# Feed-forward matmuls of 362 columns over three PSUM banks instead of 272 columns over two

## What is computed

```python
for l in range(DEPTH):                                   # 2 layers
    xp = xp + 0.5 * swiglu(rms_norm(xp, ffn1_norm[l]), *f1)
    ...                                                  # even or odd mixer
    xp = xp + 0.5 * swiglu(rms_norm(xp, ffn2_norm[l]), *f2)
# swiglu(h, gate, up, down) = (silu(h @ gate) * (h @ up)) @ down, with 1024 x 2816 and 2816 x 1024 weights
```

## Time and profile before

| | |
|---|---|
| time, 3 runs | 2167.08 us median, 2164.73 to 2167.14 |
| span of the profiled execution (the page records no time beside it) | 2169.2 us |
| TensorE busy | 2121.6 us, 98% |
| VectorE, ScalarE, GpSimd busy | 1028.8, 690.9, 274.7 us |
| chain that ended last: TensorE's share | 92%, line 646 87% |
| matmuls, each with a weight load | 16662 |

### The profile page before, as it was taken

One profiled execution on the slowest core, in us unless ns is written; L12 is line 12 of the kernel. 1 busy time (PEld: TensorE's weight loads), 2 busy tenths in 40 slices (PEclk: granted clock), 3 DMA queues, 4 the chain that ended last, 5 costly groups with the idle time before them and its releaser, 6 DMA issues.

```text
span 2169.2 us, 41417 instructions
## 1 busy us (share of the span) xinstructions
PE 2121.6 (98%) x16662; PEld 2040.0 (94%) x16662; DVE 1028.8 (47%) x1300; ACT 690.9 (32%) x908; POOL 274.7 (13%) x290
## 2 busy tenths in 40 slices
PE   9999999999999999999999999999988899999997
PEld 8999999997999999999999999999844799999997
DVE  6442444567654324455442444656835364424443
ACT  5221222237254212224441222222334244412221
POOL 0000111300310000021000001403145320000012
PEclk9999999999999999999999999999999999999999
DMA  3222432222132222222222222322589322222221
GB/s 143 87 96 79 131 108 94 91 69 73 69 107 89 91 83 88 89 93 71 86 102 83 78 90 96 112 91 83 153 236 267 117 85 87 102 82 78 87 100 68
DMA packets 68710, 218.65 MB, mean 101 GB/s; under 512 B 10186, under 2 KB 22645, under 8 KB 68544
## 3 DMA queue, kind: packets, MB, share of 16 engines
q1 hardware_dynamic: 58864, 191.00, 26.2%
q0 software_dynamic: 9184, 24.80, 4.1%
q10 hardware_dynamic: 576, 1.67, 0.2%
HBM read 212.67 MB, written 5.78 MB: 101 GB/s over the span
## 4 chain that ended last, share of the span: by engine, by line
PE 92%; DVE 3%; ACT 1%; DMA 1%; issue 1%; SPq 1%; DVEq 0%; ACTq 0%
PE ps L646 87%; PE ps L1067 1%; DVE rinv L1543 1%; DMA keys<-pool_kt 1%; DVE w_lo L1533 1%; PE ps L1094 1%; SPq L523 0%; PE ps L999 0%; ACT prob L1311 0%; DMA x<-xT 0%; PE ps L974 0%; PE ps L665 0%; PE ps L949 0%; PE ps L986 0%; PE ps L960 0%
## 5 line engine op out<-in xcount | busy, mean ns | idle before, releaser
L1210 ACT ACTIVATE w_hi<-raw 128x1024 fp32r<-128x1024 f32 (+2 forms) x298 | 334.8, 1124 | 1181.4 <-PE ps L646 1173.4
L646 PE MATMUL ps<-hx_hi,w_hi 128*128 128x272 f32 x3376 | 702.6, 289 | 5.1 <-DVE w_lo L1533 2.9
L646 PE MATMUL ps<-hx_hi,w_lo 128*128 128x272 f32 x3376 | 699.5, 289 | 0.0
L646 PE MATMUL ps<-hx_lo,w_hi 128*128 128x272 f32 x3376 | 696.9, 288 | 0.0
L646 PEld LDWEIGHTS ps<-hx_hi,w_hi 128*128 128x128 f32 x3376 | 531.8, 188 | 9.9 <-issue 5.8
L646 PEld LDWEIGHTS ps<-hx_lo,w_hi 128*128 128x128 f32 x3376 | 531.5, 189 | 0.0
L646 PEld LDWEIGHTS ps<-hx_hi,w_lo 128*128 128x128 f32 x3376 | 527.8, 189 | 0.0
L1533 DVE TENSOR_TENSOR w_lo<-raw,w_hi 128x1024 fp32r<-128x1024 f32 (+2 forms) x298 | 421.1, 1413 | 97.0 <-ACT w_hi L1210 96.7
L646 PE MATMUL ps<-hid_hi,w_hi 128*128 128x272 f32 x1408 | 291.1, 288 | 0.0
L646 PE MATMUL ps<-hid_lo,w_hi 128*128 128x272 f32 x1408 | 290.9, 288 | 0.0
L646 PE MATMUL ps<-hid_hi,w_lo 128*128 128x272 f32 x1408 | 290.8, 288 | 0.0
(11 more groups left out here) (315 smaller groups left out, 1516.5 us busy)
## 6 DMA issues: line engine op xcount, KB each, us to landing
raw<-gu SPq DMA_DIRECT2D x175, 512.0 KB, 3.2
raw<-down SPq DMA_DIRECT2D x64, 704.0 KB, 4.0
keys<-pool_kt SPq DMA_DIRECT2D x128, 144.0 KB, 4.5
vals<-pool_v POOLq DMA_DIRECT2D x128, 128.0 KB, 4.7
raw<-odd_in SPq DMA_DIRECT2D x21, 512.0 KB, 3.2
raw<-even_in SPq DMA_DIRECT2D x14, 512.0 KB, 3.2
raw<-even_out SPq DMA_DIRECT2D x8, 512.0 KB, 3.2
raw<-odd_out SPq DMA_DIRECT2D x8, 512.0 KB, 3.9
```

Of the source, the lines that this page charges most:

```text
L646: last = pe.matmul(acc[slot][0:m, a, 0:TH], w, r[:, t, a * TH:(a + 1) * TH], start=(begin and t == tiles[0] and one == 0), stop=((end if s ...
L1210: act.activation(w_hi[slot][:, 0:cols], raw[slot][:, 0:cols], ACT.Copy).then_inc(w_hi_done, 1)
```

## The change

The upper and the lower input lie side by side in one tile of 1088 columns (`hx`, `hid`, `mix`, `cq`). In the feed-forwards `wide_panel` replaces `panel`: the upper weights are multiplied with these 1088 columns in three matmuls of 362, 362 and 364 columns over three banks, the lower weights with the 544 upper columns in two of 272 as before. The sum of upper weights times lower input, and the lower weights' share of the second half of the tokens, thus end in columns of their own ("lower"), and are added when the accumulator is read: 180 columns of the second bank and 364 of the third (6 for slot 0, 7 for slot 1). For gate and up ScalarE copies the lower sum to SBUF (`copy_low`, two activations), VectorE adds upper and lower, and `rinv` is applied in passes of its own: to `gate`, and to `silu` in place of `up`. For a down panel VectorE adds to x in three passes (`wide_add_to_x`). The mixers keep `panel`, with the same matmuls, on the joined tiles. The distance matmul of the first feed-forward moves from bank 7 to bank 4 and waits for the first root.

```diff
+BANK = 512
+PIECE = 362
...
-        hx_hi = place("hx_hi", [P, DT, T], F32R)
-        hx_lo = place("hx_lo", [P, DT, T], F32R)
+        hx = place("hx", [P, DT, 2 * T], F32R)
+        hx_hi, hx_lo = hx[:, :, 0:T], hx[:, :, T:2 * T]
...
+        pieces = [(ps[:, 2 * s, BANK - PIECE:BANK], ps[:, 2 * s + 1, 0:PIECE], ps[:, 6 + s, 0:2 * T - 2 * PIECE]) for s in range(2)]
+        upper = [ps_flat[:, (2 * s + 1) * BANK - PIECE:(2 * s + 1) * BANK - PIECE + T] for s in range(2)]
+        lower = [(ps[:, 2 * s + 1, T - PIECE:PIECE], ps[:, 6 + s, 0:2 * T - 2 * PIECE]) for s in range(2)]
+        LOWER = 2 * PIECE - T
...
+            def wide_panel(n, slot, rhs, tiles, wait_input=None, begin=True, end=True, first=False):
...
+                one, two, three = pieces[slot]
+                for t in tiles:
...
+                    pe.matmul(one, hi, rhs[:, t, 0:PIECE], start=opens, stop=False)
+                    pe.matmul(two, hi, rhs[:, t, PIECE:2 * PIECE], start=opens, stop=closes)
+                    pe.matmul(three, hi, rhs[:, t, 2 * PIECE:2 * T], start=opens, stop=False)
+                    pe.matmul(one[:, 0:TH], lo, rhs[:, t, 0:TH], start=False, stop=closes)
+                    last = pe.matmul(three[:, T + TH - 2 * PIECE:2 * T - 2 * PIECE], lo, rhs[:, t, TH:T], start=False, stop=closes)
...
-                        panel(n0, n0 % 2, hx_hi, hx_lo, range(DT), split_input, first=(f == 0))
+                        wide_panel(n0, n0 % 2, hx, range(DT), split_input, first=(f == 0))
...
                 pe.wait_ge(rel_landed, 32)
-                pe.matmul(ps[:, 7, 0:3 * WIN], rel[:], onehot[:], start=True, stop=True).then_inc(dist_ready, 1)
+                pe.wait_ge(rms_done, stat(0))
+                pe.matmul(ps[:, 4, 0:3 * WIN], rel[:], onehot[:], start=True, stop=True).then_inc(dist_ready, 1)
...
+            def copy_low(out, n, slot, done):
+
+                act.wait_ge(panel_done, n + 1)
+                act.activation(out[:, 0:LOWER], lower[slot][0], ACT.Copy)
+                act.activation(out[:, LOWER:T], lower[slot][1], ACT.Copy).then_inc(done, 1)
...
                 act.wait_ge(prod_ready, 1)
                 act.activation(hid_hi[:, 0, :], prod[:], ACT.Copy).then_inc(hid_hi_done, 1)
-                act.wait_ge(acc_read, 3)
+                copy_low(gate_low, 2, 0, gate_low_done)
+                act.wait_ge(gate_ready, 2)
                 act.activation(silu[:], gate[:], ACT.Silu).then_inc(silu_done, 1)
+                copy_low(up_low, 3, 1, up_low_done)
...
                     def tile(i, cols):
+                        copy_low(gate_low, n0 + 2 * i, n0 % 2, gate_low_done)
                         split_hi(n0 + 2 * i + 2, n0 % 2, cols)
-                        act.wait_ge(acc_read, n0 + 2 * i + 1)
+                        act.wait_ge(gate_ready, h0 + i + 1)
                         act.activation(silu[:], gate[:], ACT.Silu).then_inc(silu_done, 1)
+                        copy_low(up_low, n0 + 2 * i + 1, (n0 + 1) % 2, up_low_done)
...
+            def gathered(out, low, n, slot, low_done, count):
+
+                dve.wait_ge(low_done, count)
+                dve.tensor_tensor(out[:], upper[slot], low[:], ALU.add).then_inc(acc_read, 1)
+                dve.wait_ge(acc_read, n + 1)
+
+            def scale_silu(h):
+
+                dve.wait_ge(silu_done, h + 1)
+                dve.tensor_tensor(silu[:], silu[:], rinv[:], ALU.mult).then_inc(silu_scaled, 1)
+                dve.wait_ge(silu_scaled, h + 1)
+
+            def wide_add_to_x(n, slot, m, factor, k):
...
+                dve.scalar_tensor_tensor(out=xm, in0=upper[slot], scalar=factor, in1=xm, op0=ALU.mult, op1=ALU.add).then_inc(x_upper, 1)
+                dve.wait_ge(x_upper, k + 1)
+                dve.scalar_tensor_tensor(out=xm[:, 0:LOWER], in0=first, scalar=factor, in1=xm[:, 0:LOWER], op0=ALU.mult, op1=ALU.add)
+                dve.scalar_tensor_tensor(out=xm[:, LOWER:T], in0=second, scalar=factor, in1=xm[:, LOWER:T], op0=ALU.mult, op1=ALU.add)\
+                   .then_inc(acc_read, 1)
...
-                        dve.wait_ge(panel_done, n0 + 2 * i + 1)
-                        dve.tensor_tensor(halves(gate[:]), acc_of(n0 % 2), halves(rinv[:]), ALU.mult).then_inc(acc_read, 1)
+                        gathered(gate, gate_low, n0 + 2 * i, n0 % 2, gate_low_done, h0 + i + 1)
+                        dve.tensor_tensor(gate[:], gate[:], rinv[:], ALU.mult).then_inc(gate_ready, 1)
                         split_lo(n0 + 2 * i + 2, n0 % 2, cols)
-                        dve.wait_ge(panel_done, n0 + 2 * i + 2)
-                        dve.tensor_tensor(halves(up[:]), acc_of((n0 + 1) % 2), halves(rinv[:]), ALU.mult).then_inc(acc_read, 1)
-                        dve.wait_ge(silu_done, h0 + i + 1)
-                        dve.wait_ge(acc_read, n0 + 2 * i + 2)
+                        scale_silu(h0 + i)
+                        gathered(up, up_low, n0 + 2 * i + 1, (n0 + 1) % 2, up_low_done, h0 + i + 1)
                         dve.tensor_tensor(prod[:], up[:], silu[:], ALU.mult).then_inc(prod_ready, 1)
```

More of the change, by code:

```diff
@@ L696, in ffn @@
                         for s in range(2):
-                            panel(n0 + 2 * i + s, (n0 + s) % 2, hx_hi, hx_lo, range(DT))
+                            wide_panel(n0 + 2 * i + s, (n0 + s) % 2, hx, range(DT))
                     if f == 0 and c == 0:
@@ L703, in hidden @@
                         pe.wait_ge(hid_done, done + t + 1)
[L704 to L705 removed]
+                    wide_panel(n1, n1 % 2, hid, range(FT), hidden)
+                    wide_panel(n1 + 1, (n1 + 1) % 2, hid, range(FT))
                     with pe.Fori(1, DT // 2) as i:
                         for s in range(2):
[L708 removed]
+                            wide_panel(n1 + 2 * i + s, (n1 + s) % 2, hid, range(FT))
             def mixer_out_begin(start, tiles, pieces, which=(0, 1)):
@@ L713, in mixer_out_begin @@
                 for t in which:
-                    panel(start + t, (start + t) % 2, mix_hi, mix_lo, tiles, end=False)
+                    panel(start + t, (start + t) % 2, mix, tiles, end=False)
             def mixer_out(start, early, late, pieces, token_halves=(0, 1)):
@@ L897, in even @@
                     if k < 0:
-                        panel(n, n % 2, hx_hi, hx_lo, range(DT), split_input if t == 0 else None)
+                        panel(n, n % 2, hx, range(DT), split_input if t == 0 else None)
                     else:
-                        panel(n, n % 2, hx_hi, hx_lo, range(DT // 2), end=False)
+                        panel(n, n % 2, hx, range(DT // 2), end=False)
                         unit_score(k)
@@ L903, in even @@
                             unit_values(k - 2)
-                        panel(n, n % 2, hx_hi, hx_lo, range(DT // 2, DT), begin=False)
+                        panel(n, n % 2, hx, range(DT // 2, DT), begin=False)
                         if k >= 1:
@@ L1164, in split_cq @@
                         pe.wait_ge(cq_done, t + 1)
-                    panel(n, n % 2, cq_hi, cq_lo, range(QT), split_cq if h == 0 else None)
+                    panel(n, n % 2, cq, range(QT), split_cq if h == 0 else None)
                     if h == 0:
```

109 lines of the change are left out of this document (64 added, 45 removed).

## The result

| | before | after |
|---|---|---|
| median | 2165.9 us (4 runs, 2164.3 to 2167.14) | 2192.71 us (4 runs, 2188.89 to 2195.16) |
| span of the profiled execution | 2169.2 us | 2193.2 us |

The ratio is 1.0117, 95% interval 1.0096 to 1.0139: the changed kernel is slower by 1.2%, where I had forecast 0.8% faster, and 16 us above the range.

A forecast was written before the change was run, and what follows sets the result against it. TensorE, 98% busy, was taken as the bound. Fewer matmuls saving 25.1 us and stalls adding 7.3 us gave -17.8 us off the median of 2167.08, so 2149.3 us; range 2143 to 2177.

The forecast's parts named there:

- The count and the place: Whole kernel: TensorE is the bound; 2112 feed-forward tiles each go from six matmuls to five with the same 1632 columns.
- Slack in the loops: Steady gate and up panels: the added VectorE and ScalarE work costs nothing, with 2.2 us to spare.
- the down panels' three passes: Down panels: one VectorE pass of 0.72 us becomes three, about 1.6 us, within 8.3 us, costing nothing.
- I take the first: Feed-forward tiles: 11.9 ns fixed per matmul, so one fewer saves 25.1 us over 2112 tiles; chance 0.48.
- a wide matmul that starts off a good address: Wide feed-forward matmuls: one costing more than its columns would make the prediction wrong; no size or chance given.
- rival 1: Feed-forward matmuls: cost is per column, nothing saved, stalls left, 2174.4 us; slower from 165.8 ns per wide matmul; chance 0.23.
- Rival 2: Feed-forward matmuls: mostly per column, small fixed part; at 3 ns 6.3 us saved, 2168.1 us; chance 0.20.
- rival 3: Feed-forward matmuls: none follows the last in under 125.2 ns; 100.3 us saved, 2074 us; chance 0.06.
- (a): First feed-forward, run-in: panel 2's read waits behind product, `hid_hi` and `copy_low`; TensorE stalls about 2.6 us.
- (b): Start of the other three feed-forwards: an add goes before the scaling, TensorE waits longer for `w_lo`; 2.5 us in all.
- (c): Last down panel of the first three feed-forwards: later x delays `hx_lo` for the next panel; 1.3 us in all.
- (d): End of the kernel: the chain runs through the last, longer add to x; 0.9 us.

## Why the prediction was wrong, step by step

**The count and the place.** 2112 tiles, five matmuls instead of six, TensorE the bound: right. Slack in the loops, the down panels' three passes: right, no steady panel waits.

**The price of a matmul: wrong, and nearly the whole miss.** The step was "I take the first", a fixed 11.9 ns per matmul and columns at 2.4 GHz, tile 739.3. Measured is 759.9. The tile was to lose 11.9 ns and gained 7.7: 19.6 ns x 2112 = 41.4 us, against a miss of 2192.7 - 2149.3 = 43.4. Counted from 739.3 the error is 20.6 ns and has two parts; 1 ns of it is that the tile before measures 752.2, not 751.2. The other 2 us of the miss lie in the stalls, the mixers and the spread between executions.

- *Mis-sized fixed part.* It is some 2.5 ns (0 to 3), the rest of the 11.9 is about 0.45 ns per column instead of 0.417. That lifts 739.3 to 746.2, 14.6 us. I had split 125.2 ns with nothing but rows of 272 columns and two arguments. The half clock could not tell: in the stretch from 40.8 to 44.2 a tile takes 1360 ns, which is 1632/1.2, and the wide matmul that takes 171.8 at full clock is within 3 ns of N/1.2 (304.5 against 301.7). A feed that is slow only above 1.2 GHz is hidden there just like a fixed piece of work, as the prediction itself said. And plain fp32 matmuls take their columns at half the rate, so their law says nothing of a feed near one column per cycle. Both reasons fitted both cases, and I gave one of them 0.48.
- *The cuts.* Pieces that begin at 362 and 724 cost 13.7 ns a tile over those 746, 28.9 us. The prediction named this ("a wide matmul that starts off a good address") only as something that would make it wrong, with no price and no chance, though the trace before has a hint: its 272-column spacings are uneven, mostly 122 to 127 ns, while all their inputs begin at multiples of 16 columns of the tile.

**Rivals.** The deciding point of rival 1 held: slower from 165.8 ns per wide matmul on; the three average 167.8. Its price was too low, since it kept the tile at 751.2. Rival 2, mostly per column with a small fixed part, is nearest to what the runs show where the cuts are harmless: 2168 was its time, 2167.62 the run with cuts at 366 and 718. That these agree so closely is partly luck, for the tile of that run saves 5.4 ns and not 3. By the rule of the Trainium skill ("TensorE: Matmul & The Clock Gate", section "Wait — 56ns, not 53.3ns?") a matmul less is worth 2.5 ns. Here five matmuls in place of six gave between 5.4 ns a tile less and 7.7 more, so no run shows that figure by itself. A floor as in rival 3 shows at some 110 ns, where it decides nothing for 272 columns or more.

**Stalls.** (a) 2.6 forecast; 2.1 measured, by the chain that was named, and 1.7 more for the half clock behind it, which was not foreseen. Another 1.7 of the run-in's 6.0 are like it: a stretch of 3.4 us at 1.2 GHz from 13.5 on, which half of the fourteen profiles lack, that of the kernel before among them. (b) 0.8 each forecast, 0.7 measured (1.25 against 0.55 of waiting). (c) 1.3 forecast; nothing measured where no mixer lies between: from the end of the second feed-forward's last down panel to TensorE's wait in the third 12.88 us before, 12.93 after. (d) 0.9 forecast, 0.8 measured. In sum 7.3 forecast, 6.3 (2 to 8) between the medians with nearly equal tiles. That the sums are close is partly luck: the 1.3 of (c) did not come, and the half clock was in no term.

**What the range missed.** It ended at rival 1. The sum of a feed per column and of a bad place for the cuts was possible from the rows, and no bound was put on it.

## What to carry to other kernels

Merging matmuls saves the fixed part of each, and that has to be measured at two widths before it is multiplied by thousands: with one width in a trace, a surplus per matmul and a surplus per column look the same, and a slower clock that hides it tells nothing. When an operand is cut anew, look at each position's spacing by itself and try two or three cuts: here moving them by 4 and 6 columns moved a tile by 13 ns, more than the matmul that was saved. Before a difference of a few ns is read as a cause, look at whether the mean is one level or a mixture of two. A stall of 2 us in front of TensorE can cost nearly twice its length, by the clock granted behind it; the order of short steps on the other engines is worth a look there.
